# First block's attention: the scores of two steps ahead moved behind a step's dense pieces

## The reference, cut to what matters

```python
s_cmp = jnp.einsum('bghsd,bgnd->bghsn', q, kc)          # compressed keys
o_cmp = jnp.einsum('bghsn,bgnd->bghsd', p_cmp.astype(vc.dtype), vc)
...
s = jnp.einsum('bghqd,bgqnkd->bghqnk', qb, kb)          # selected keys (all 8 of 8 blocks)
p = masked_softmax(s, m)
...
s = jnp.einsum('bghqd,bgkd->bghqk', qb, kb)             # window
p = masked_softmax(s, m)
...
o = gt[..., 0:1] * o_cmp + gt[..., 1:2] * o_slc + gt[..., 2:3] * o_win
```

## Time and profile before

| what | value |
|---|---|
| median of 3 runs | 3364.55 us (3364.12 to 3364.76) |
| the profiled execution | 3364.42 us, span 3362.5 us |
| PE busy | 3316.0 us, 99% |
| DVE busy | 1821.4 us, 54% |
| ACT busy | 1241.0 us, 37% |
| chain that ended last | PE 90%, DVE 4%, ACT 3% |

### The profile page before, as it was taken

One profiled execution on the slowest core, in us unless ns is written; L12 is line 12 of the kernel. 1 busy time (PEld: TensorE's weight loads), 2 busy tenths in 40 slices (PEclk: granted clock), 3 DMA queues, 4 the chain that ended last, 5 costly groups with the idle time before them and its releaser, 6 DMA issues.

```text
span 3362.5 us, 43205 instructions
## 1 busy us (share of the span) xinstructions
PE 3316.0 (99%) x16894; PEld 2646.3 (79%) x16894; DVE 1821.4 (54%) x2948; ACT 1241.0 (37%) x1882; POOL 331.9 (10%) x242
## 2 busy tenths in 40 slices
PE   8999999999999999999999999999999999999999
PEld 7667888776788878888777778888888876788887
DVE  6776333667743446443666664436644367654436
ACT  3354222425542324332333342324423235532325
POOL 0310000221100020000223100000000012000001
PEclk9999999999999999999999999999999999999999
DMA  4112222321133222223322122233222321132332
GB/s 165 63 45 76 97 97 95 130 66 49 45 107 100 94 100 82 94 100 107 103 73 68 67 83 99 94 106 103 83 95 97 103 97 45 57 105 95 100 107 82
DMA packets 81433, 300.39 MB, mean 89 GB/s; under 512 B 9040, under 2 KB 9040, under 8 KB 80640
## 3 DMA queue, kind: packets, MB, share of 16 engines
q1 hardware_dynamic: 78624, 284.20, 25.3%
q0 software_dynamic: 1568, 11.98, 0.9%
q10 hardware_dynamic: 1088, 2.10, 0.2%
HBM read 296.14 MB, written 2.10 MB: 89 GB/s over the span
## 4 chain that ended last, share of the span: by engine, by line
PE 90%; DVE 4%; ACT 3%; issue 1%; POOL 1%; DMA 0%; POOLq 0%; ACTq 0%; DVEq 0%
PE bank L913 26%; PE bank L915 25%; PE bank L914 25%; PE bank L957 2%; PE bank L964 2%; PE bank L958 2%; DVE wl L2146 1%; PE bank L1241 1%; PE bank L1222 1%; ACT wh L1645 1%; PE bank L1482 1%; PE bank L1494 1%; PE bank L1537 1%; ACT sc L1817 1%; PE bank L1256 1%
## 5 line engine op out<-in xcount | busy, mean ns | idle before, releaser
L913 PE MATMUL bank<-x,wh 128*128 128x512 f32 x2616 | 1044.1, 399 | 4.2 <-DVE wl L2146 2.9
L915 PE MATMUL bank<-x,wl 128*128 128x512 f32 x2616 | 1020.0, 390 | 0.0
L914 PE MATMUL bank<-x,wh 128*128 128x512 f32 x2616 | 1019.0, 390 | 0.0
L1645 ACT ACTIVATE wh<-raw 128x1024 fp32r<-128x1024 f32 x526 | 555.8, 1057 | 1116.7 <-PE bank L915 1066.0
L2146 DVE TENSOR_TENSOR wl<-raw,wh 128x1024 fp32r<-128x1024 f32 x526 | 671.8, 1278 | 531.8 <-ACT wh L1645 530.7
L913 PEld LDWEIGHTS bank<-x,wh 128*128 128x128 f32 x2616 | 491.3, 188 | 124.0 <-issue 22.6
L915 PEld LDWEIGHTS bank<-x,wl 128*128 128x128 f32 x2616 | 491.1, 188 | 103.8
L914 PEld LDWEIGHTS bank<-x,wh 128*128 128x128 f32 x2616 | 491.8, 188 | 99.4 <-issue 3.8
L913 PE MATMUL bank<-mid,wh 128*128 128x512 f32 x1216 | 474.9, 391 | 0.5 <-DVE wl L2146 0.5
L915 PE MATMUL bank<-mid,wl 128*128 128x512 f32 x1216 | 473.1, 389 | 0.0
L914 PE MATMUL bank<-mid,wh 128*128 128x512 f32 x1216 | 473.1, 389 | 0.0
(11 more groups left out here) (377 smaller groups left out, 3329.7 us busy)
## 6 DMA issues: line engine op xcount, KB each, us to landing
raw<-stream SPq DMA_DIRECT2D x526, 512.0 KB, 3.3
raw_apart<-stream SPq DMA_DIRECT2D x12, 512.0 KB, 3.5
sm<-small POOLq DMA_DIRECT2D x2, 2144.0 KB, 10.4
tb<-tab POOLq DMA_DIRECT2D x2, 1728.0 KB, 14.6
h<-x_t ACTq DMA_DIRECT2D x4, 512.0 KB, 6.7
out_t<-h SPq DMA_DIRECT2D x8, 256.0 KB, 2.7
tba<-tab_a POOLq DMA_DIRECT2D x1, 1152.0 KB, 7.7
pf<-p_t POOLq DMA_DIRECT2D x2, 512.0 KB, 5.1
```

Of the source, the lines that this page charges most:

```text
L913: pe.matmul(dst, hi, src[:, kc, 0, :], start=start, stop=False)
L914: pe.matmul(dst, hi, src[:, kc, 1, :], start=False, stop=False)
L915: return pe.matmul(dst, lo, src[:, kc, 0, :], start=False, stop=stop)
L1645: act.activation(high_of(n)[:, :], raw_of(n)[:, :], ACT.Copy).then_inc(hi_done, 1)
```

## The change

The entry "scores s+2" and the dense pieces of `take` change places, in steps 0 to 9 of both layers. No instruction is added or removed. ACT, POOL and SP keep their orders; PE and DVE change theirs.

```diff
--- before.py
+++ after.py
@@ -249,9 +249,9 @@
                 yield from parts[len(parts) * n // len(groups):len(parts) * (n + 1) // len(groups)]
         if s < 11:
             yield "norm", s + 1
+        yield from take((4, 3, 3 if s == 10 else 2, 4 if s < 11 else 1)[t])
         if s < 10:
             yield "scores", s + 2
-        yield from take((4, 3, 3 if s == 10 else 2, 4 if s < 11 else 1)[t])
         yield "values", s
         if s == 8:
             yield "exps", (10, 0)
```

## The result

The changed kernel takes 3377.48 us (median of 6 runs, 3376.80 to 3378.88), the kernel before 3364.66 us (6 runs, 3364.12 to 3365.24). The ratio is 1.0039, 95% interval 1.0029 to 1.0049: slower by 12.8 us. The forecast was 3375.5 us, 3368.5 to 3381.5.

What follows compares the result with a forecast made beforehand. PE, busy 99%, was taken to bound the kernel. New waits less saved seams gave +5.5 us per layer, +11.0 on 3364.42, so 3375.4; with 0.1 for the median, 3375.5 us, range 3368.5 to 3381.5.

Steps and rivals of the forecast that it cites:

- The seams: On PE, one array-shape change fewer per step saves 0.16 us, -3.2 us over 20 steps, bounds -6.4 and 0.
- Step 0: Three DVE instructions go ahead of reading scores 2; PE waits 0.75 us for norm 2 at blocks (2, 0).
- Steps 1 and 2: Norm 3 is 0.9 us late; then late `nm` 4 holds up ACT's copy, PE waits 2.7 us at (3, 2).
- Step 5: `nm` 7 is put at +4.3 us; the copy behind its exponential delays blocks (6, 2) from +2.9 to +4.3.
- D: Lateness of a moment against the kernel before, in the first layer; forecast to end at +5.5 us per layer.
- Step 8: Scores 10 end later; the shift copy behind step 10's first exponential makes blocks (9, 0) late, +5.6 us.
- the third rival: PE's clock falls in step 3 behind the 2.7 us wait: 0 to +8.3 us per layer, 3381 us; chance 0.10.
- its doubling: One layer's sum counts twice; this fails if the second layer differs from the first by over 0.5 us.
- The slack is enough: Rival: ACT copies blocks (3, 1) before step 4's exponential, no new waits: -3.2 us, 3361.3 us; chance 0.07.
- Only half of it: Rival: only step 2's 2.7 us wait stays, +1.1 to +3.5 per layer, 3367 to 3371.5 us; chance 0.15.
- the four places: New PE waits: 0.7 us at blocks (2, 0), 2.7 in step 3, over 1.5 in step 6, over 1 at (9, 0).

Runs made afterwards that it cites:

- with fillers: Changed kernel with 10 more filler matmuls ahead of blocks (3, 2) and 8 ahead of blocks (6, 2), computing nothing: 3375.53 us, ratio 1.0033.
- PE alone: Kernel before, with only PE taking pieces ahead of scores in steps 0 to 9, DVE keeping its order: 3369.15 us, ratio 1.0015.
- step 2 put back: Changed kernel with the old order restored in step 2 only, on PE and DVE: 3372.48 us, ratio 1.0025.
- exponentials of step 4: Changed kernel with the first two exponentials of step 4 moved later in ACT's order, behind copies: 3372.65 us, ratio 1.0025.
- with step 6 and the shift: The run with step 4's exponentials moved, plus step 7's first behind the copy of (6, 1) and the shift copy ahead of step 10's first: 3369.16 us.
- DVE alone: Kernel before, with only DVE taking the new order in steps 0 to 9, PE keeping scores ahead of pieces: 3387.65 us, ratio 1.0068.

## Why the prediction was right

The sign, the mechanism and the places were right; one term was missing from the sum.

*The seams.* Forecast 0.16 us per step, measured 0.21 in step 0 and 0.17 to 0.20 in the others that no wait disturbs (1, 4, 7 and 9). The seam of scores into values, which no row had shown, costs what scores into pieces did: in the changed kernel the 384-wide scores start at 158.37 and the values at 159.86, 1.49 us later; before, scores at 155.85 and the piece at 157.34, also 1.49 us. The rule of the Trainium skill that the prediction cites, in "TensorEngine Tiling (Array Packing)" under Key Properties, that a change of the tiling mode drains the array, agrees with that; by that rule alone the kernel would have gained.

*Step 0.* `nm` 2 was to start its instruction so as to end at 164.0, 1.7 us of it reaching norm 2, and PE to wait 0.75 us. The rows have `nm` 2 at 163.59 to 163.76, with all of that kernel 0.23 us early (blocks (0, 0) at 153.81 against 154.04), and a wait of 0.80 us.

*Steps 1 and 2.* +0.9 at (3, 0) was +0.94. The new wait of 2.7 us was 2.49 us, and ACT waited 3.06 us ahead of it.

*Step 5.* D from +2.9 to +4.3 at blocks (6, 2): with fillers it goes from +2.90 at (6, 0) to +4.33 at (7, 0), and `nm` 7 itself is +4.3 late. The prediction puts this +4.3 without a sum that leads to it, so of step 5 the wait is foreseen with its reason, and its size less so.

*Step 8.* The copy of the shift behind an exponential was worth +1.1 us, from +4.49 at (8, 0) to +5.62 at (9, 0) with fillers; I had put +1.3 from +4.3 on. That both ways give +5.6 is two misses of 0.2 us that cancel.

*What was off.* The sum was +11.0 us, the fillers' profile gives 5.41 + 5.40 = +10.8. The rest of the +12.8 is the third rival, the clock, which I had given 0.10 and should have added: about 2 us in the median and 3.9 in the profiled execution. I had argued that nothing in the rows showed a fall; but the rows held no wait of this length in this stretch, so they could not speak against it. The bounds (0 and +8.3 per layer) held. Against the run with fillers (the table) the changed kernel lost 1.5 us by the fall in step 3 of the first layer, 1.4 us by the one of the second, and 1.1 us up to blocks (7, 0) by the one in step 6 of the second, of which 0.7 us are left at the end of the layer, where it has no wait for norm 7 any more. The clock is also why the layers differ, by 0.9 us at blocks (7, 0) and 0.5 us at the end, which is the border that the prediction set to its doubling; with fillers they agree to 0.02 us. In Part 1 of "TensorE: Matmul & The Clock Gate" the Trainium skill says that idleness halves this clock; the rows agree, with 0.50 behind the wait of 2.49 us in both layers. That the forecast came within 2 us of the median is in part luck: in executions like the profiled one the missing term is 3.9 us.

*The other rivals.* "The slack is enough" fell with the 3.06 us at ACT. "Only half of it" fell as well: every one of the four places took nearly its full price. In the runs with parts of the change, though, the sums were too low four times by 2 to 5 us (PE alone 3.2, step 2 put back 2.0, exponentials of step 4 2.7, and with step 6 and the shift 4.7) and once by 10 (DVE alone), mostly for one reason: I had looked at who stands behind DVE in the loop of the scores, and not at the pieces that wait for L2162 and L2539, nor at the score banks that wait to be read. In the run of DVE alone the clock is about half of the miss; in the run with fillers, 2.2 us above its forecast, the clock had cost the median less than the profiled execution.

## What to carry to other kernels

When one plan gives the order to several engines, moving an entry moves it on each of them, and the cost may lie on an engine that is half idle: here all of PE's gain was a seam of 0.2 us per step, and DVE's four instructions ahead of the row maxima cost 2.5 us on PE in step 2 of each layer. The move has a price on the leading engine too: with PE alone in the new order 5 of the 13 us were still lost. Ask what stands next in the queue of the engine that is made to wait: the 0.6 us copy behind the exponential was what PE needed, and moving the exponentials of one step took 5 of the 13 us away. A wait of about 2 us in a matmul stretch can have a second price, the clock, 1.1 to 1.5 us for each fall here; fill it or add it to the sum.

## What the runs showed of the hardware that was not expected

The granted clock fell to 1.2 GHz behind a wait of 2.49 us, although PE ran 8 short filler matmuls just ahead of it, and behind one of 1.78 us in one layer but not behind one of 1.80 us in the other. Ahead of the one of 1.78 us PE had been busy without a gap (4.00 of 4.00 us from 838 to 842, 2.00 of 2.00 us from 842 to 844). Ten executions of one kernel with one such wait in each layer fell into two groups 1.8 us apart. So nearly the same wait costs its clock in one place and not in the other, and probably in some executions and not in others; a kernel with such waits shows a wider spread (2.1 us against 0.7 us with fillers). Ten filler matmuls in a wait of 2.5 us kept the clock at 1.00 and did not delay the blocks behind it.
